# Strassen products for one up projection, a router on column groups, and constant products at the gathers

## What is computed

```python
def expert_choice_ffn(h, w_router, w_gate, w_up, w_down):
    cap = CAPACITY_FACTOR * S // N_EXPERTS              # 128
    logits = jnp.einsum('bsd,de->bse', h, w_router).astype(jnp.float32)
    aff = jax.nn.softmax(logits, axis=-1)
    gate, idx = lax.top_k(aff.transpose(0, 2, 1), cap)
    xe = jax.vmap(lambda hb, ib: hb[ib])(h, idx)
    ...

def conv_glu_ffn(h, w_up, conv_w, conv_b, w_down):      # D_FF = 2816, w_up: 1024 x 5632
    gate, val = jnp.split(h @ w_up, 2, axis=-1)
    gate = causal_dwconv(gate, conv_w, conv_b)          # three taps
    return (jax.nn.silu(gate) * val) @ w_down
```

## Time and profile before

| | us |
|---|---|
| median of 3 runs | 4317.2 (4314.47 to 4317.55) |
| profiled execution | 4317.77 |
| its span, first to last instruction | 4316.0 |
| TensorE busy | 4046.4 (94%) |
| VectorE busy | 1459.2 (34%) |
| ScalarE busy | 825.9 (19%) |
| GpSimd busy | 130.0 (3%) |
| mean granted TensorE clock | 0.976 |

### The profile page before, as it was taken

One profiled execution on the slowest core, in us unless ns is written; L12 is line 12 of the kernel. 1 busy time (PEld: TensorE's weight loads), 2 busy tenths in 40 slices (PEclk: granted clock), 3 DMA queues, 4 the chain that ended last, 5 costly groups with the idle time before them and its releaser, 6 DMA issues. The chain is left out here.

```text
span 4316.0 us, 36999 instructions
## 1 busy us (share of the span) xinstructions
PE 4046.4 (94%) x15260; PEld 1974.7 (46%) x15260; DVE 1459.2 (34%) x2003; ACT 825.9 (19%) x1582; POOL 130.0 (3%) x122
## 2 busy tenths in 40 slices
PE   7989977999998999995999999799989999999999
PEld 3444443444443544452444444444575444444444
DVE  6878442111111687524111111255442211111001
ACT  2154311101011234321101010233341100000000
POOL 0000000000000000000000000000120000000000
PEclk9999988999999999997999999999999999999999
DMA  8210138999995201116999997211001111111110
GB/s 286 73 40 1 57 123 320 354 346 349 349 347 163 86 0 40 40 59 254 358 344 353 346 351 274 86 34 35 26 23 69 44 59 54 39 39 39 49 59 34
DMA packets 252869, 647.57 MB, mean 150 GB/s; under 512 B 16544, under 2 KB 103200, under 8 KB 252704
## 3 DMA queue, kind: packets, MB, share of 16 engines
q1 hardware_dynamic: 243200, 611.66, 39.4%
q0 software_dynamic: 9504, 33.56, 3.2%
HBM read 603.22 MB, written 41.94 MB: 149 GB/s over the span
## 5 line engine op out<-in xcount | busy, mean ns | idle before, releaser
L1545 PE MATMUL ps<-w_ring,h_act 128*128 128x512 f32 x3008 | 1307.3, 595 | 13.4 <-ACT h_act L1639 12.1
L1545 PEld LDWEIGHTS ps<-w_ring,h_act 128*128 128x128 f32 x3008 | 570.1, 191 | 723.9 <-issue 703.6
L3005 PE MATMUL ps<-h_act,arena_two 128*128 128x512 f32 x1408 | 604.6, 592 | 0.0
L3005 PEld LDWEIGHTS ps<-h_act,arena_two 128*128 128x128 f32 x1408 | 267.4, 190 | 336.3 <-issue 336.3
L896 DVE SCALAR_TENSOR_TENSOR y<-y,par_one 128x1024 f32<-128x1024 f32 x240 | 307.5, 1281 | 3.9
L3063 PE MATMUL ps<-arena_two 128*128 128x512 f32 x704 | 302.3, 592 | 0.0
L1685 DVE SCALAR_TENSOR_TENSOR h_act<-ps,gate,gate_row 128x1024 f32<-128x1024 f32 x30 | 38.5, 1284 | 746.3 <-PE ps L1545 746.3
L1627 ACT ACTIVATE h_act<-ps 128x1024 f32<-128x1024 f32 x32 | 32.8, 1025 | 1178.6 <-PE ps L1545 1178.6
L1970 PE MATMUL ps<-h_act,arena_two 128*128 128x512 f32 x544 | 235.8, 594 | 1.3 <-DVE h_act L390 1.0
L568 PE MATMUL ps<-h_act,arena_a 128*128 128x512 f32 x512 | 221.5, 593 | 4.2 <-DVE h_act L390 2.0
L3063 PEld LDWEIGHTS ps<-arena_two 128*128 128x128 f32 x704 | 133.8, 190 | 168.4 <-issue 168.4
(11 more groups left out here) (410 smaller groups left out, 3786.6 us busy)
## 6 DMA issues: line engine op xcount, KB each, us to landing
w_ring<-in_w_gate SPq DMA_DIRECT2D x128, 1024.0 KB, 8.3
w_ring<-in_w_up SPq DMA_DIRECT2D x128, 1024.0 KB, 7.0
w_ring<-in_w_down SPq DMA_DIRECT2D x128, 1024.0 KB, 5.2
w_mod<-in_w_ada SPq DMA_DIRECT2D x48, 512.0 KB, 6.5
w_mod<-in_w_mod SPq DMA_DIRECT2D x48, 512.0 KB, 6.6
arena_two<-in_ffn_w_up SPq DMA_DIRECT2D x44, 512.0 KB, 5.1
arena_b<-in_w_ada SPq DMA_DIRECT2D x32, 512.0 KB, 4.4
arena_two<-in_ffn_w_down SPq DMA_DIRECT2D x22, 512.0 KB, 5.6
```

Source lines behind the costliest of these rows:

```text
L1545: last = nc.tensor.matmul(ps[:, bank + i, :], lhs[:, k * P:(k + 1) * P], ring[:, c, k % kp, i * HALF:(i + 1) * HALF], start=(k == 0), stop ...
L3005: last = nc.tensor.matmul(ps[:, 4 * (j % 2) + 2 * which + half, :], z.w_up[j % 2][:, which, k, :], h[:, k, half * HALF:(half + 1) * HALF], ...
```

## The change

**Up projections.** Weights are loaded in 22 sets of 1 MB: 256 channels of the gate, then the same 256 of up, and so on (n = 0 to 21). With the weights A (256 rows of output channels by 1024) and h (1024 channels by 1024 tokens) cut into 2 by 2 blocks, a set is seven products M1 to M7 in place of eight, each four matmuls (K = 512) into one bank, banks in turn. The sums of weights S1, S2, A11 - A21 and S4 are made by GpSimd for each set; the sums of h, T1 to T4, by VectorE once, at the beginning. ScalarE copies M1 out; VectorE adds the rest up into the four output blocks (`combine`), then makes the convolutions on `hid` itself and multiplies. Down weights and x are loaded into other places, later; x comes back in eight transfers.

**LRU gates and pair sums**: `by_corners` goes; two matmuls with the whole 128 by 128 matrix in its place.

**Router**: the weights, padded to 32 columns, are the stationary operand; the turned tile (128 columns) moves. Of the eight matmuls four go to each half of the sum, one into each column group of 32 (`score_parts`); ScalarE copies the 128 by 128 result (`keep_parts`), and one matmul with a constant folds the four groups into the logits (`score`). The load of ScalarE's exp table after the last tile is put ahead of `keep_parts`.

**Constant products**: four matmuls of a constant matrix by constants, after the lists are turned and before the wait for the tokens.

```diff
+def keep_awake(core, bank, n):
...
+    for _ in range(n):
+        core.nc.tensor.matmul(core.ps[:, bank, :], core.c("ident", P), core.con[:, 0:HALF], start=True, stop=True)
...
                     for k in range(KD):
-                        last = nc.tensor.matmul(logits[t], xT[t % 2][:, k * P:(k + 1) * P], wr[:, k, :],
-                                                start=(k == 0), stop=(k == KD - 1))
-                    last.then_inc(logits_made, 1)
+                        g = k % 4
+                        last = nc.tensor.matmul(partial[t][g * GROUP:(g + 1) * GROUP, :], wr[:, k, :], xT[t % 2][:, k * P:(k + 1) * P],
+                                                start=(k < 4), stop=(k >= 4))
+                    last.then_inc(parts_made, 1)
+
+                def score(t):
+                    pe.wait_ge(parts_kept, t + 1)
+                    nc.tensor.matmul(logits[t], parts[:, t % 2, :], core.c("fold", N_EXP), start=True, stop=True).then_inc(logits_made, 1)
...
                         elif (t, k) == (3, 4):
+                            score_parts(0)
+                            turn_row(1)
+                        elif (t, k) == (3, 5):
                             score(0)
-                            turn_row(1)
                         elif (t, k) == (3, 6):
+                            score_parts(1)
+                            turn_row(2)
+                        elif (t, k) == (3, 7):
                             score(1)
-                            turn_row(2)
                         elif (t, k) == (4, 0):
+                            score_parts(2)
+                        elif (t, k) == (4, 1):
                             score(2)
                         elif k == 2:
                             turn_row(t - 1)
                         elif k == 4:
+                            score_parts(t - 1)
+                        elif k == 5:
                             score(t - 1)
...
+                def keep_parts(t):
+                    act.wait_ge(parts_made, t + 1)
+                    nc.scalar.activation(parts[:, t % 2, :], partial[t], ACT.Copy).then_inc(parts_kept, 1)
...
                     keep_turned(t)
+                    if t == QT - 1:
+                        act.wait_ge(tables, 3)
+                        nc.scalar.activation(warm, bias[:, 0:1], ACT.Exp, scale=0.0).then_inc(tables, 1)
+                    keep_parts(t)
...
+                nc.vector.memset(wr[:, :, N_EXP:], 0.0).then_inc(padded, 1)
...
                 nc.tensor.matmul(other, core.c("turn", P), lists[:, :, N_EXP:], start=True, stop=True).then_inc(turned_back, 1)
+                keep_awake(core, 5, 4)
                 pe.wait_ge(chosen, 5)
...
-                        by_corners(claim_pair(what, k), z.gates[:, g, k, :], lru_xc[k % 2]).then_inc(gates_ready, 1)
+                        b = claim_pair(what, k)
+                        for i in range(NH):
+                            last = nc.tensor.matmul(ps[:, b + i, :], z.gates[:, g, k, :], lru_xc[k % 2][:, i * HALF:(i + 1) * HALF],
+                                                    start=True, stop=True)
+                        last.then_inc(gates_ready, 1)
...
+                def up(n):
+                    sp.dma_start(z.up_slots[n % 2], up_k[:, :, n % 2, (n // 2) * 2 * P:(n // 2 + 1) * 2 * P]).then_inc(up_landed[n % 2], 16)
...
+                for n in range(2, n_sets):
+                    sp.wait_ge(m4_done, n - 1)
+                    up(n)
+                sp.wait_ge(stored, 16 * QT)
+                sp.wait_ge(m4_done, n_sets - 1)
+                down(0, 0)
+                down(1, 0)
+                sp.wait_ge(m1_done, n_sets)
+                down(2, 0)
+                down(3, 0)
...
+                sp.wait_ge(m5_done, n_sets)
+                down(9, 0)
+                down(10, 0)
+                sp.wait_ge(m4_done, n_sets)
+                sp.wait_ge(hid_made, 4 * n_pairs)
+                for t in range(QT):
+                    sp.dma_start(last_x[t], x_rows[t * P:(t + 1) * P, :]).then_inc(x_again, 16)
...
+                def sums(n):
+                    a11, a12, a21, a22 = a_block(n, 0, 0), a_block(n, 0, 1), a_block(n, 1, 0), a_block(n, 1, 1)
+                    pool.wait_ge(up_landed[n % 2], 16 * (n // 2 + 1))
+                    if n:
+                        pool.wait_ge(m5_done, n)
+                        pool.wait_ge(s_made, 4 * n)
+                    nc.gpsimd.tensor_tensor(s1, a21, a22, ALU.add).then_inc(s_made, 1)
+                    if n:
+                        pool.wait_ge(m6_done, n)
+                    pool.wait_ge(s_made, 4 * n + 1)
+                    nc.gpsimd.tensor_tensor(s2, s1, a11, ALU.subtract).then_inc(s_made, 1)
+                    nc.gpsimd.tensor_tensor(a21, a11, a21, ALU.subtract).then_inc(s_made, 1)
+                    if n:
+                        pool.wait_ge(m3_done, n)
+                    pool.wait_ge(s_made, 4 * n + 3)
+                    nc.gpsimd.tensor_tensor(s4, a12, s2, ALU.subtract).then_inc(s_made, 1)
...
+                def block_product(n, kind, left, right, each=None):
+                    q = 7 * n + kind
+                    if kind and n:
+                        pe.wait_ge(read[kind - 1], n)
+                    elif n >= 2:
+                        pe.wait_ge(read[M4], n - 1)
+                    for k in range(KH):
+                        if each is not None:
+                            pe.wait_ge(each, k + 1)
+                        last = nc.tensor.matmul(ps[:, q % 8, :], left[:, k, :], right[k], start=k == 0, stop=k == KH - 1)
+                    return last
...
-                up_half(0, 0, 0)
+                m1(0)
+                m2(0)
                 turn(1)
                 pe.wait_ge(weighed, QT)
-                up_half(0, 1, 0)
+                m1(1)
                 pe.wait_ge(kept_act, 8)
                 pe.wait_ge(kept_dve, 8)
...
+                for n in range(n_sets):
+                    if n >= 2:
+                        m1(n)
+                    if n:
+                        m2(n)
+                    m6(n)
+                    m7(n)
+                    m5(n)
+                    m3(n)
+                    m4(n)
...
+                    dve.wait_ge(m1_kept, n + 1)
+                    dve.wait_ge(m2_done, n + 1)
+                    add(c11_made, c11, z.m1, M2)
+                    then(0, 0, first_half, c11)
+                    dve.wait_ge(m6_done, n + 1)
+                    add(u2_made, z.u2, z.m1, M6)
+                    dve.wait_ge(m7_done, n + 1)
+                    add(u3_made, z.u3, z.u2, M7)
+                    dve.wait_ge(m5_done, n + 1)
+                    add(c22_made, c22, z.u3, M5)
+                    add(u4_made, z.u2, z.u2, M5)
+                    then(1, 1, second, c22)
+                    dve.wait_ge(m3_done, n + 1)
+                    add(c12_made, c12, z.u2, M3)
+                    then(2, 0, second, c12)
+                    dve.wait_ge(m4_done, n + 1)
+                    add(c21_made, c21, z.u3, M4)
+                    then(3, 1, first_half, c21)
...
+                dve.wait_ge(kept_act, 8)
+                dve.wait_ge(kept_dve, 8)
+                dve.wait_ge(grouped, QT)
+                for k in range(KH):
+                    differences(z.t1, b12, b11, t1_made, k)
+                    dve.wait_ge(t1_made, k + 1)
+                    differences(z.t2, b22, z.t1, t2_made, k)
+                for k in range(KH):
+                    differences(b12, b22, b12, t3_made, k)
+                dve.wait_ge(stored, 16 * QT)
+                dve.wait_ge(t2_made, KH)
+                for k in range(KH):
+                    differences(z.t4, b21, z.t2, t4_made, k)
...
+                for p in range(n_pairs):
+                    gates(p)
+                    conv(p, 0)
+                    conv(p, 1)
+                    ups(p)
```

More of the change, by code:

```diff
@@ L1184, in constants_row @@
                     for k in range(KD):
-                        last = nc.tensor.matmul(constant, shifts[:, k, :], wr[:, k, :], start=(k == 0), stop=(k == KD - 1))
+                        last = nc.tensor.matmul(constant, shifts[:, k, :], routers[:, k, :], start=(k == 0), stop=(k == KD - 1))
                     last.then_inc(constant_made, 1)
@@ L1807, in __init__, with rows @@
[L1807 to L1811 removed]
+        def rows(at, n, size=HALF):
+            return [everything[:, at + i * size:at + (i + 1) * size] for i in range(n)]
@@ new lines, in __init__ @@
+        spare = core.gates2[:, 1 - DEPTH % 2, :]
+        self.m1, self.u3 = (spare[:, i * HALF:(i + 1) * HALF] for i in range(2))
+        self.u2, self.v = (core.gate1[:, i * HALF:(i + 1) * HALF] for i in range(2))
+        halves = [core.h[:, i:i + n, half * HALF:(half + 1) * HALF] for i, n, half in ((0, 2, 0), (2, 2, 0), (4, 2, 0), (0, 2, 1), (2, 2, 1))]
+        two = [everything[:, x:x + S].rearrange("p (k n) -> p k n", k=2)
```

(37 more changed lines are left out.)

227 lines of the change are left out of this document (139 added, 88 removed).

## The result

The changed kernel takes 4223.9 us (median of 4 executions, 4218.1 to 4225.2), the one before 4317.4 (4, 4314.5 to 4318.2): a ratio of 0.978, 95% interval 0.977 to 0.980. That is 93.5 us less, where 91.5 were forecast, and inside the range. The 93.5 are uncertain by some 6 us to either side.

What follows compares the result with a forecast made beforehand. TensorE, behind itself in block two's up and down projections, was taken as the bound. -75.5 + 2.6 - 1.7 - 9.6 - 1.6 - 5.7 = -91.5, so 4317.2 - 91.5 = 4226 us; range 4215 to 4246.

Steps and rivals of the forecast that it cites:

- The bound (1): Block two's up projections: seven products for eight, 88 matmuls fewer at 0.858 us each, -75.5 us.
- What lies beside (1): Up projections: VectorE, ScalarE, GpSimd's sums and weight loads fit beside a set of 24.0 us; nothing taken for it.
- rivals by which GpSimd sets the pace: Block two: GpSimd's sums bound sets in part, 4248 us (0.05), to about no change (0.01), or slower (0.02).
- The first set (2): Start of up projections: M6 and M7 wait for VectorE's T2 and T3, 0.7 and 1.9 us late, +2.6 us.
- the upper end of 4.3: First set of up projections: the wait costs 4.3 us if the clock falls as well, 1.7 us of matmuls lost.
- The end of the stage (3): End of up projections: down weights, last hidden rows and returning x all arrive in time, 0 us.
- Corners (4): LRU gates and pair sums: two whole matmuls for four corner ones, twelve times 0.14 us, -1.7 us.
- Router (5): Router scores: column groups abreast, 0.90 us for 1.70, seven times a layer; with late waits -9.6 us, ends -14 and +7.3.
- The two late waits: Router, t = 3 and t = 2: VectorE's score, row scale and copy end 0.4 us late each, +0.8 us a layer.
- The zeroing of the padding: Router: costs 0.1 us on VectorE ahead of the first statistics, left inside the router's ends.
- The last score (6): Before the choice of tokens: table load, copy, fold and score in line, 2.7 us; -1.6 us, ends -3 and +2.
- The gathers (7): After the lists: constant matmuls raise the clock earlier, -3.4 and -2.3, together -5.7 us; ends -7.1 and +1.4.

Runs made afterwards that it cites:

- number 1: Kernel before with only block two's Strassen up projections changed; router, gathers and corners as they were: 4244.6 us, ratio 0.983.
- number 6: Changed kernel with six more GpSimd sums in each set (the first one repeated), ten for four: 4227.6 us, ratio 0.979.
- number 7: Changed kernel with sixteen more GpSimd sums in each set (the first one repeated), twenty for four: 4570.3 us in one execution.
- number 5: Changed kernel with M2 of set 1 moved ahead of set 0's M6: 4218.4 us, ratio 0.977.
- number 3: Changed kernel without the four constant matmuls at each gather: 4229.4 us, ratio 0.979.
- number 8: Changed kernel with M2 of set 1 ahead of set 0's M6 and three constant matmuls before the last tile's turn: 4222.0 us, ratio 0.978.
- number 4: Changed kernel with all eight router matmuls of a tile in one column group instead of four: 4248.0 us, ratio 0.983.

## Why the prediction was right, point by point

**The bound (1).** Right in its place and size. Sets are 24.03 us for the 24.0 worked out, and number 1 shows that the gain doesn't depend on the rest. Distances from start to start carried it: by the 592 ns that the page gives for a record, 88 products would have been 104 us.

**What lies beside (1).** Right: no wait in 21 sets for a sum, a bank's reader or the weights. The estimate for a sum, 1.15 us scaled from 384 columns, was 10% low: alone it takes 1.27, from start to start 1.23 to 1.41. The worst, 2.22, stayed under the 2.8 allowed. VectorE's load was worked out as 20.2 us for a pair of sets of 48.1; over 200 us from 3640 it is busy for 83.0, so 20.0. One step was wrong without a price: M6 was said to come four products after M5, which doesn't hold for set 1, where it is three (number 6). The four sums fit there too; ten miss it by 1.8 us, once.

Of the rivals by which GpSimd sets the pace, numbers 6 and 7 show the mechanism, with other terms. Their extra sums all stand ahead of the second one, so what ties there is that sum and then M6, M7 and M5, in series: 37.5 to 41 us a set in number 7, and not the time of its twenty sums, some 28. Four sums that are all slow alike, which is what the prediction priced (7.1 us each for no change), were not tried.

The traces show what the two engines cost each other. Beside GpSimd's sums a VectorE subtraction of two SBUF rows took up to 1.75 us for 0.69 (number 6) and a multiplication of two as much (number 7); an addition with a PSUM input stayed at 0.69 (number 7), and the four sums of a set with three such additions among them at 1.26 to 1.27 (after, from 3633.87). An operation with one SBUF row suffers too: the row scale of 1024 columns took 1.58 us beside GpSimd's first sums, for 0.75 in the kernel before, where GpSimd is idle there. The sum beside it and beside a VectorE addition of two SBUF rows took 2.22. VectorE's timeline of after, and GpSimd's:

```profile
3372.62 1.58 DVE L342 TENSOR_SCALAR arena_two<-arena_two,squares 128x1024 f32<-128x1024 f32 x1
```

```profile
3371.43 2.22 POOL L3098 TENSOR_TENSOR arena_two<-arena_two 128x512 f32<-128x512 f32 x1
```

Here it costs nothing, since TensorE has M1 and M2 over it: from the first product to the transposes' end it is 10.84 us, as before.

**The first set (2).** Predicted 2.6 us, found 2.26 (number 5 against after), where M6 and M7 were said to wait, released by VectorE's differences. The 0.2 taken for a signal is what the kernel before shows from TensorE to ScalarE (turn's end 537.58, copy 537.78); from VectorE's eighth subtraction to M6's matmul after it is 0.06 us (3387.17 to 3387.23). The fall of the clock that the upper end of 4.3 allowed didn't come: the granted clock is 1.00 from 3372 to 3400.

**The end of the stage (3).** Right: the down product's 704 records take 302.15 us in one piece, as before.

**Corners (4).** Predicted -1.7, found -2.0; two whole matmuls take 1.72 us (2922.68 to 2924.40) for the four corners' 1.86, and the piece behind them is 0.1 to 0.2 shorter too (13.83 for 13.93 and 27.47 for 27.67).

**Router (5).** The cost of a score held: 0.90 us all told, since a tile's turn went from 16.40 to 15.60. Its terms divide otherwise: the parts 0.57 for 0.69, the fold 0.14 (535.76 to 535.90) for 0.21, and the other 0.19 lies in neither. It shows in the projections next to them: 1.82 us for 1.72 behind the parts of later tiles (568.46 to 570.28). That it is the changes of shape is my reading. The two late waits were sized too high, at 0.8 us a layer: from the first score to the last turn 82.20 us became 77.06, 5.14 less, where 7 x 0.80 = 5.60 would be without any wait, so they cost 0.46. One of them shows by name, 0.23 us for VectorE's copy, which the prediction named. The zeroing of the padding, put at 0.1 us, takes VectorE 0.17.

**The last score (6).** The order was right (table load, copy, fold, score in line), and from load to score it is 2.36 us for the 2.7 of the sum; the copy takes 0.26 for 0.36. The terms were -1.06 and -0.45, 1.5 together and not the 1.6 of the sum; the traces give -1.88 and -0.76. Most of the 1.88 isn't the edit's. In the profiled execution of before, TensorE fell to the lower clock while it turned the last tile of layer 0 (granted clock 0.72 from 617 to 618, 0.50 behind it), so the turning took 1.75 us and the table load started 2.40 us after the turn; after, the turning took 1.09 and the load came at 1.95. With the old score and a turning at the whole clock (before in layer 1, number 1 in both) it is 4.90 to 5.09 us from turn to VectorE's score, and 4.31 now. So the edit gives 0.6 to 0.8 us a layer, 1.2 to 1.6 in all, for 1.6 predicted; the rest of the 2.6 is where the clock happened to fall.

**The gathers (7).** Right in kind, 1.4 us too small. Two terms: the constants were to end 0.5 and 0.9 us after the tokens, and ended before them in layer 0 (0.23 us of idle), because the clock rose within them, at 658 to 660; so the gate product ran at the whole clock from its first record, 13.8 us in both layers, where half of the loss was kept in the sum.

**What offset what.** Nothing: each of the five stretches gave more than its term, by 0.3 to 1.4 us, 3.8 in all, of which about 1 is the clock in the last score. The medians give 2.0 more than the sum. Their difference is uncertain by some 6 us, so that closeness is in part luck; what carries the prediction is the up stage, 73.3 us for 72.9.

## What to carry to other kernels

Where the chain of waits is one engine behind itself, price an edit by the distance from start to start of its records and test each helper against the length of the new period; there the forecast was good to 1 us in 73. A helper on GpSimd has to be placed in time against VectorE's operations on SBUF, since both slowed down here (0.69 to 1.75 us for a subtraction, 1.27 to 2.22 for a sum), and the periods to look at are the first two, where the order of the products differs. And idle time of TensorE can cost twice, by its length and by the clock after it. The next set's product put into it gave back the length (2.26 us, number 5, where the clock hadn't fallen); constant products give back only the clock (3.6 and 3.4 us, number 3), and little where another engine ends last (number 8).

## What the runs showed of the hardware

- VectorE and GpSimd on SBUF together: a subtraction of two SBUF rows of 512 columns 0.69 us alone and 1.18 to 1.75 beside GpSimd (number 6), a row scale 0.75 (before) and 1.58 (after), a GpSimd sum 1.27 and up to 2.22 (after). An addition with a PSUM input stayed at 0.69 (number 7), and a set's four sums with three such additions among them at 1.26 to 1.27 (after).
- Sixteen records of 32 columns in four column groups take 0.57 us (after), in one group 1.87 (number 4).
- Whole matmuls in place of the four 64 by 64 corners save less where the neighbour is a tile of another shape: with the 64 by 128 tiles ahead of them 3.73 us for 3.78, else 1.72 for 1.86 (before and after).
- TensorE after a wait of 15 us for GpSimd: its next 8 records took 5.18 us where 3.43 is due, and the granted clock was 0.68 over the 6 us from 3610 (number 7).
